# First modulation by chunks of channels, with the first weight slots worked between them

## The reference

```python
silu_c, silu_cc = silu(c), silu(c_ctx)
mod   = silu_c  @ ada_w[0] + ada_b[0]        # for the 256 tokens of x
mod_c = silu_cc @ ada_w[0] + ada_b[0]        # for the 256 tokens of ctx
sh_m, sc_m, g_m, sh_f, sc_f, g_f = split(mod, 6)
h  = rmsnorm(x,   norm_mix_w[0]) * (1 + sc_m)  + sh_m
hc = rmsnorm(ctx, norm_mix_w[0]) * (1 + scc_m) + shc_m
p, pc = h @ ab_w_in, hc @ ab_w_in            # 1024 -> 2560: u, v, q, k, v of the attention
...
k_mem, v_mem = mem @ xa_w_k[0], mem @ xa_w_v[0]    # used by a later layer
```

## Time and profile before

| | us |
|---|---|
| median of three runs | 2557.49 |
| the profiled execution's own time | 2559.29 |
| its span in the trace | 2557.3 |
| TensorE busy | 2496.8 |
| VectorE busy | 1989.3 |
| ScalarE busy | 1175.6 |

### The profile page before, as it was taken

How to read it: one execution, slowest core, us unless ns; L and a number is a source line. 1 busy time by engine, 2 the same in 40 slices (tenths; PEclk the granted TensorE clock), 3 DMA queues, 4 the chain that set the end, 5 groups by cost and what they waited for, 6 DMA issues and landing times.

```text
span 2557.3 us, 41955 instructions
## 1 busy us (share of the span) xinstructions
PE 2496.8 (98%) x16459; PEld 2145.1 (84%) x16459; DVE 1989.3 (78%) x2455; ACT 1175.6 (46%) x1498; POOL 89.2 (3%) x116
## 2 busy tenths in 40 slices
PE   7999999999999999999999899999999999999998
PEld 5877788888889998889999688888888888888886
DVE  2886877777767886757887748888888888988887
ACT  3435200001421005531014736777777777777776
POOL 0100100000000001000002000000000000000000
PEclk8999999999999999999999999999999999999999
DMA  8843444453335553334554035999899989999996
GB/s 333 313 168 126 167 172 167 167 172 116 116 108 218 181 180 141 108 108 160 185 181 185 16 115 194 374 363 374 334 375 366 366 340 373 366 351 357 364 373 252
DMA packets 91397, 602.74 MB, mean 236 GB/s; under 512 B 9840, under 2 KB 12912, under 8 KB 24688
## 3 DMA queue, kind: packets, MB, share of 16 engines
q1 hardware_dynamic: 76848, 540.05, 55.9%
q0 software_dynamic: 14400, 60.56, 6.7%
HBM read 598.47 MB, written 2.10 MB: 235 GB/s over the span
## 4 chain that ended last, share of the span: by engine, by line
PE 92%; DVE 4%; ACT 2%; issue 1%; DMA 1%; SPq 0%; DVEq 0%; ACTq 0%
PE bank L1188 12%; PE bank L1191 12%; PE bank L1192 12%; PE bank L2492 8%; PE bank L2496 8%; PE bank L2495 8%; PE bank L2527 4%; PE bank L2523 4%; PE bank L2526 4%; PE bank L535 2%; PE bank L1425 1%; PE bank L1446 1%; ACT arena L1470 1%; PE bank L2505 1%; PE bank L1176 1%; PE bank L1238 1%
## 5 line engine op out<-in xcount | busy, mean ns | idle before, releaser
L984 DVE TENSOR_TENSOR ring_part<-ring,arena_part 128x2048 fp32r<-128x2048 f32 x481 | 1079.9, 2274 | 29.7 <-ACT arena_part L1003 13.5
L2848 ACT ACTIVATE arena_part<-ring 128x2048 fp32r<-128x2048 f32 x339 | 647.0, 1920 | 192.7 <-DMA ring<-in_stream 192.4
L1188 PE MATMUL bank<-arena_part 128*128 128x256 f32 (+1 forms) x2040 | 652.2, 320 | 7.6 <-DVE ring_part L984 7.6
L1192 PE MATMUL bank<-arena_part,ring_part 128*128 128x256 f32 (+1 forms) x2040 | 648.6, 318 | 0.0
L1191 PE MATMUL bank<-h_part,arena_part 128*128 128x256 f32 (+1 forms) x1496 | 474.9, 317 | 0.0
L1188 PEld LDWEIGHTS bank<-arena_part 128*128 128x128 f32 x2040 | 390.7, 192 | 38.0 <-issue 11.3
L1192 PEld LDWEIGHTS bank<-arena_part,ring_part 128*128 128x128 f32 x2040 | 390.6, 191 | 25.8
L2492 PE MATMUL bank<-arena_part,h_part 128*128 128x512 f32 x896 | 354.2, 395 | 0.0
L2496 PE MATMUL bank<-arena_part,h_part 128*128 128x512 f32 x896 | 349.6, 390 | 0.0
L2495 PE MATMUL bank<-ring_part,h_part 128*128 128x512 f32 x896 | 348.9, 389 | 0.0
L1292 ACT ACTIVATE arena<-bank 128x256 f32<-128x256 f32 (+1 forms) x66 | 30.1, 456 | 636.6 <-PE bank L1192 635.6
(11 more groups left out here) (376 smaller groups left out, 3071.2 us busy)
## 6 DMA issues: line engine op xcount, KB each, us to landing
ring<-in_stream SPq DMA_DIRECT2D x511, 1024.0 KB, 4.9
arena<-in_ada_stream POOLq DMA_DIRECT2D x80, 512.0 KB, 4.4
consts<-in_mem_w POOLq DMA_DIRECT2D x8, 512.0 KB, 4.1
consts<-in_small POOLq DMA_DIRECT2D x1, 2800.0 KB, 11.7
arena<-in_c_rows POOLq DMA_DIRECT2D x2, 1024.0 KB, 6.9
arena<-in_ab_bias POOLq DMA_DIRECT2D x1, 2048.0 KB, 8.5
arena<-in_t_bias POOLq DMA_DIRECT2D x1, 2048.0 KB, 7.9
arena<-in_mem_t SPq DMA_DIRECT2D x1, 1024.0 KB, 4.9
```

Source lines behind the costliest of these rows:

```text
L984: return nc.vector.tensor_tensor(low, value, high.bitcast(F32), ALU.subtract)
L1188: m = nc.tensor.matmul(out_ap, w_high, high, start=start, stop=False)
L1192: return nc.tensor.matmul(out_ap, w_low, high, start=False, stop=stop)
L2848: nc.scalar.activation(high, ring[:, where], ACT.Copy).then_inc(sem("moe_high"), 1)
```

## The change

- `START` has only K0a, K0b, V0a, V0b. The 8 MB of shift and scale weights are laid out anew, `ada_mix`: one MB for each 128 *output* channels of shift and of scale together, with all 1024 input channels. SP loads them into ring rooms 0 to 3 behind AB0 and AB1, each behind a wait of its own.
- `ada_products(c)` makes shift and scale of one chunk of channels: eight matmuls of 256 columns with 32 stationary columns (two used, the rest zero). ScalarE copies the bank out (`copy_rows`), `fold_rows(c)` adds the four groups and turns them in two small matmuls with the constant `fold`, and VectorE's `first_scale(c)` adds the bias and makes the scale.
- `first_products(k)` does the 96 matmuls of AB0 and AB1 with the four output tiles side by side, twelve matmuls for each chunk, between `ada_products(c + 3)` and `fold_rows(c + 2)` of later chunks.
- Rounding and splitting of AB0 and AB1 comes before the modulation, that of AB2 and AB3 stands amid the eight chunks. The 24 later chunks are spread over AB4 to AB9. The memory values use banks 4 and 5 and are copied out earlier.

The pieces of the diff stand in the order TensorE, ScalarE, VectorE, SP.

```diff
-START = ["K0a", "A0", "A1", "K0b", "A2", "A3", "V0a", "A4", "A5", "V0b", "A6", "A7"]
+START = ["K0a", "K0b", "V0a", "V0b"]
...
+            mem_value_products()
...
+            for c in range(DC):
+                pe.wait_ge(sem("squared"), bk.up("squared"))
+                m = group_sums(sums, sqv[:, c, :], TT, c == 0, c == DC - 1)
+            m.then_inc(full(sums), 1)
+            ada_products(0)
+            ada_products(1)
             mem_value_products()
+            fold_rows(0)
             rstd_pe(bk, TT)
+            fold_rows(1)
+            ada_products(2)
...
+            for c in range(DC):
+                if c + 3 < DC:
+                    ada_products(c + 3)
+                if c + 2 < DC:
+                    fold_rows(c + 2)
+                first_products(c)
...
+            for c in range(DC):
+                if c + 3 < DC:
+                    copy_rows(c + 3)
+                for s in range(2):
+                    t = slice(SEQ * s, SEQ * (s + 1))
+                    scaled_act(bk, c == DC - 1 and s == 1, spread_last)
+                    nc.scalar.activation(ab_high[:, c, t], hv[:, c, t], ACT.Identity, bias=shift(0, 0, c, s))\
+                        .then_inc(sem("in_high"), 1)
+                if c in (3, 5):
+                    slot_high_act(bk, AB_AT + 2 + (c == 5), ab_slot_high, fresh=True)
...
+                if c in (4, 6):
+                    slot_low_dve(bk, AB_AT + 2 + (c == 6), ab_slot_high)
...
-            for n in range(2, 7):
-                first_chunks(3 * n - 6, 3 * n - 3)
+            for n, chunks in ((4, (0, 5)), (5, (5, 9)), (6, (9, 12))):
+                first_chunks(*chunks)
                 slot_low_dve(bk, AB_AT + n, ab_slot_high)
...
+            for n in range(2, RING):
+                load(n)
+            for j in range(DC):
+                if j >= ADA_ROOMS:
+                    sp.wait_ge(*marks["ada_made"][j - ADA_ROOMS])
+                elif j == ADA_ROOMS - 1:
+                    for made in marks["values_full"]:
+                        sp.wait_ge(*made)
+                else:
+                    sp.wait_ge(sem("slots_used"), j + 2)
```

More of the change, by code:

```diff
@@ L1919, in _, with ada_products, fold_rows @@
             pe.wait_ge(sem("silu_c_ready"), 1)
[L1921 to L1935, removed]
             pe.wait_ge(sem("mem_split"), DC)
             mem_key_products(range(2, 4))
-            ada_products(2)
+            mem_value_products()
+            rows_copied, ada_made = [], []
+            marks["ada_made"] = ada_made
+            def ada_products(c):
+                b = bk.fill(ADA_BANKS[c % 2])
+                rows_copied.append(bk.freed(bk.turn - 1))
+                pe.wait_ge(free(b), bk.emptied())
+                pe.wait_ge(sem(f"ada_landed{c % ADA_ROOMS}"), 16 * (c // ADA_ROOMS + 1))
+                room = ring[:, c % ADA_ROOMS * SLOT:(c % ADA_ROOMS + 1) * SLOT]
+                for late in range(2):
+                    for g in range(4):
+                        k = 4 * late + g
+                        m = nc.tensor.matmul(PS[b][32 * g:32 * g + 32, X2], silu_c[:, k, :],
+                                             room[:, k * SEQ:(k + 1) * SEQ], start=not late, stop=bool(late))
+                m.then_inc(full(b), 1)
+                ada_made.append((full(b), bk.filled()))
+            def fold_rows(c):
+                pe.wait_ge(*rows_copied[c])
+                b = bk.fill(FOLD_BANK)
+                pe.wait_ge(free(b), bk.emptied())
+                for n in range(2):
+                    m = nc.tensor.matmul(PS[b][:, 4 * c + 2 * n:4 * c + 2 * n + 2], ada_rows[c % 4][:, n * P:(n + 1) * P],
+                                         small_at("fold")[:, 0:2], start=True, stop=True)
+                m.then_inc(full(b), 1)
+            sums = bk.next_bank()
             for c in range(DC):
@@ L1942, in _ @@
             m.then_inc(full(sums), 1)
-            ada_products(3)
+            ada_products(0)
+            ada_products(1)
             mem_value_products()
+            marks["values_full"] = [(full(b), bk.filled_in[b]) for b in MEM_BANKS]
+            fold_rows(0)
             rstd_pe(bk, TT)
[L1946 to L1962, removed]
@@ L2618, in _, with copy_rows @@
             root_act(bk, TT, 0)
[L2619 to L2627, removed]
+            for n in range(2):
+                slot_high_act(bk, AB_AT + n, ab_slot_high, fresh=True)
+            def copy_rows(c):
+                b = bk.fill(ADA_BANKS[c % 2])
+                act.wait_ge(full(b), bk.filled())
+                nc.scalar.activation(ada_rows[c % 4], PS[b][:, X2], ACT.Copy).then_inc(free(b), 1)
+            copy_rows(0)
+            copy_rows(1)
             for n in range(4):
                 bk.fill(MEM_BANKS[n % 2])
+            b = bk.fill(MEM_BANKS[0])
+            act.wait_ge(full(b), bk.filled())
+            nc.scalar.activation(mem_made_values(0), PS[b][:, :], ACT.Copy).then_inc(free(b), 1)
+            bk.fill(MEM_BANKS[1])
+            bk.turn += 1
+            spread_last = bk.freed(bk.turn - 1)
+            copy_rows(2)
+            for c in range(DC):
[8 more added lines that the diff above has]
+                    slot_high_act(bk, AB_AT + 2 + (c == 5), ab_slot_high, fresh=True)
+            for _ in range(DC):
+                bk.fill(FOLD_BANK)
             def silu_rows(rows, times):
@@ L2645, in _ @@
                 to(uT[:, g, :], ACT.Gelu_apprx_tanh)
[L2646 to L2649, removed]
+            for n in range(4, 6):
+                slot_high_act(bk, AB_AT + n, ab_slot_high, used=AB_AT + 3)
             for t in range(4):
```

156 lines of the change are left out of this document (101 added, 55 removed).

## The result

The changed kernel takes 2567.39 us (median), the kernel before 2557.55 beside it on the same chip: the ratio is 1.0036, with a 95% interval from 1.0027 to 1.0046. That is 9.8 us slower. The profiled execution took 2569.23 us, 9.9 more than that of before.

What follows compares the result with a forecast made beforehand. TensorE was taken to bound the kernel, with VectorE's chain 1.4 us behind at the gate. Gate 2.5 us later plus 2.4 of cold clock gave +4.9: 2562.4 us against the median of 2557.5, range 2554 to 2569.

Steps and rivals of the forecast that it cites:

- the sum: Whole kernel: gate begins 2.5 us later, cold clock behind it costs 2.4, everything after as before; +4.9 us.
- rival D: Loop: POOL's 3.5 MB of loads collide with modulation chunks 5 to 7; +8.4 us, 2565.9; chance 0.08.
- rival A: Whole kernel: the sum holds, with or without either cold stretch; -3 to +8 us around +4.9; chance 0.75.
- two cold stretches: Half clock at the loop's first chunk (0 to 3.4 us, 1.7 taken) and behind the gate's wait (1.7 to 3.4, 2.4 taken).
- B: TensorE's head start reaches the end, with VectorE's chain ending 7 us sooner; -6 us, 2551.4; chance 0.10.
- C: TensorE's clock is at half through the loop, pitch 8.7 us; +15 us, 2577; chance 0.07.
- without the gap of 2.91 us it keeps the full clock: Start, K0b's products: TensorE goes on at once from K0a, so 48 matmuls at full clock end at 22.7.
- The one half-speed stretch that I did allow for: Loop's first chunk, after TensorE's idling from 41.7 to 46.5: a loss between 0 and 3.4 us, 1.7 taken.
- VectorE's chain after it: 78.4: VectorE's 24 later chunks, first to last: 78.4 us against 80.6 before, with about 5 us of waiting for a chunk.
- The steps of the pitch: Each loop turn: modulation products, copy, two roundings and handoffs take 2.5 us, twelve matmuls 2.73; pitch 5.3 us.
- by it the loop would be at half speed throughout: Loop: the prediction's reading of the skill page on throttling in waiting loops, against which it set the attention's full clock.
- Costed at nothing: Third and fourth SP waits, splits from AB4 on (AB8's tightest), and moved value copies (0.6 us each): no cost.

Runs made afterwards that it cites:

- e1: Changed kernel with the gate's weights in a room of their own, loaded amid the 24 chunks, not after the last: 2559.30 us, ratio 1.0008.
- e8: Changed kernel with 18 small matmuls on constants ahead of the loop, where TensorE waits for the fourth modulation chunk: 2564.45 us, ratio 1.0030.
- e12: Changed kernel with only the portions of the 24 later chunks between VectorE's slots changed, to 4, 3, 3, 3, 4, 4, 3: 2569.48 us, ratio 1.0046.
- e5_three: Changed kernel with gate's weights loaded early, ScalarE's copy behind the rounding, and `silu_rows` moved behind the fifth chunk's rounding: 2554.92 us, ratio 0.9986.
- e10_two: Changed kernel with the gate's weights loaded early and ScalarE's copy behind the rounding: 2553.04 us, ratio 0.9982.
- e2: Changed kernel with ScalarE's `copy_rows(c + 3)` behind the two roundings of chunk c, not ahead of them: 2563.92 us, ratio 1.0022.
- e11: e10_two with the 24 later chunks in portions 4, 3, 3, 3, 4, 4, 3 between VectorE's slots: 2556.21 us, ratio 0.9992.
- e3: Changed kernel with `silu_rows` moved from behind the last rounding to behind the fifth chunk's, so VectorE starts sooner: 2567.78 us, ratio 1.0043.

## Why the prediction was right, and where it was off

**The mechanism held.** The start of TensorE's stage moved forward, that of VectorE's back, and the gate's weights, loaded behind VectorE's last chunk, became the wait. e1 shows it: with the weights early and nothing else changed, 7.6 us come back. The size did not hold: the sum said +4.9, and it was +9.4, nearly twice as much. That the time lies in the range (to 2569) is partly luck, since the range was widened for rival D, which did not occur; rival A, the sum, was given 2556 to 2567 and in other places at most +8 or +8.5, and its own two cold stretches at their longest add only 2.7 to the 4.9. One sign failed as well: the gate's matmuls were to begin between 163 and 168 and began at 172.58. Another held barely, the 85.8 us from VectorE's first chunk to the landed weights, where 80 to 86 were given. Rivals B, C and D did not occur as told: TensorE's head start did not reach the end (B), the loop did not run at half speed (C), and no turn behind the first waited for a modulation chunk (D). (B's price does not follow from its condition: at a pitch of 4 us the prediction's own steps put AB2 near 76 to 78, not at 81.5.)

**The sizes, in the order of the sum.**

| step | predicted | measured |
|---|---|---|
| fourth modulation chunk landed | 44.0 | 46.6 |
| first products | 46.5 | 49.90 |
| pitch of the loop | 5.3 | 5.3 (first turn 6.8) |
| AB2 begun | 83.0 | 86.35 |
| VectorE's first chunk | 83.4 | 86.70 |
| from there to the end of the last chunk | 78.4 | 81.3 |
| from there to the weights landed | 4.5 | 4.5 |
| TensorE's wait at the gate | 7 | 8.1 |
| gate's products begin | 166.3 (+2.5) | 172.58 (+8.8) |
| cold clock behind it | 2.4 | 1.7 |

Two terms were mis-sized. They add up: the start of VectorE's chain 3.3 later, the chain 2.9 longer, the cold clock 0.7 less, so 4.9 + 3.3 + 2.9 - 0.7 = 10.4, and the traces have 10.5. The first step is "without the gap of 2.91 us it keeps the full clock": that gap closed, but TensorE waited 2.10 us at V0a, and behind it the clock was 0.50 for 3.4 us. The prediction's own times hold this wait (K0b's products end at 22.7, V0a is split at 24.4), but it charges nothing for the clock behind it. This cost 1.7; together with V0a's start at 24.96 instead of 24.4 (VectorE copies a memory key out in between, L3063 at 24.44) it moved the sums and V0b, behind which SP may issue the fourth modulation chunk, and with that the whole loop. The one half-speed stretch that I did allow for came as well (1.93 for 1.07, 6.76 for 5.31: 2.3 us, where 1.7 was taken; e8's median fell by 2.5, with its share of chance). In all 3.4 us, and since VectorE's chain hangs on the loop's end they arrive at the gate in full.

The second is "VectorE's chain after it: 78.4", where the wait for chunks was put at 5 us. It was 8.4, in five places; the rest of the chain was 0.5 shorter than summed. The even portions (e12) took the waits for chunks away and the chain was no shorter, since ScalarE's rounding of AB6, which TensorE's progress sets, took their place. So the term was mis-sized because I added up VectorE's own work and one known wait. It left out the four further waits for chunks (4.5 us), and also that a slot in mid-chain has a time before which it cannot be split: in the changed kernel that rounding ended at 121.6 and VectorE came to AB6 at 122.18, so without the 3.3 us of waits for chunks ahead of it VectorE would have stood there for 2.7 of them. Behind that point the one long wait, for a chunk behind the load of constants, is 3.92 in the changed kernel and 4.8 and 5.1 in e5_three and e10_two. In e12_even that chunk was issued 12 us behind the constants (128.69, not 3 us as in the changed kernel) and VectorE did not wait for it.

**The loop.** The steps of the pitch (copy 0.46 ahead of two roundings, 1.2 us of waiting less what the fold fills) were right: 0.76 of waiting by the trace, and with the copy behind the rounding the pitch fell by 0.9. Weighed against it was the page TensorE: Matmul & The Clock Gate of the Trainium skill, section "HAM oscillation — how this bites in real kernels", whose case is a loop that waits in each turn for longer than it works and starts each turn cold. The waits here are much shorter than the work, so "by it the loop would be at half speed throughout" asked more of that page than it says. The trace of the changed kernel shows full speed (1.00 from 53 to 60) with waits of 0.76 in 5.3 us; single waits of about 2 us had a cold stretch behind them at 25 and 46.

**Costed at nothing.** SP's waits and the value copies cost nothing that shows. AB8's split was late by 1.5 and took that from the wait at the gate, as the prediction said it would; in e10_two, where that wait is gone, it is 1.9 us on the path.

**Where the head start of 13 us went.** By AB2 1.3 us were left: AB0 and AB1 with the modulation between them last 36.5 us (49.90 to 86.35), before 24.6. The groups by line (count, busy us, mean ns, idle before) for that stretch of the changed kernel:

```profile
L1981 PE MATMUL bank<-arena_part 128*128 128x512 f32 x32 | 14.2, 445 | 4.3 <-ACT arena_part L2681 4.3
...
L1937 PE MATMUL bank<-ring,rstd 128*32 128x256 f32 x64 | 4.3, 385 | 0.0
L1947 PE MATMUL bank<-consts,arena 128*128 128x2 f32 x20 | 3.0, 255 | 0.7 <-DVE mod L3091 0.7
```

The 96 matmuls at 0.23 are 21.8, the waits 4.3 and 0.7, the chunk matmuls 4.3, the folds 3.0, the cold first turn 1.5: 35.6, which leaves 0.9 of 36.5 without an account. The order alone gives back 0.9 us in each of four turns, 3.6 us, by the pitch of e2; its median fell by 3.0.

## What to carry over

When work is brought forward on one engine, follow the resource that the next meeting point waits for back to *its* engine, and see whether that engine's start moved too; here it moved the other way, and the smallest repair was to free the load from that chain (7.6 us for a few lines). A chain of one engine that takes things from others is not the sum of its own work: look for the pieces in it that something else sets, because time gained ahead of them is lost there. In e11 and e12 that was a slot's rounding (5.9 and 6.3 us of waiting), in e3 a chunk's landing (4.55 us). And in a loop that hands over each turn, what is for a later turn belongs behind what the other engine waits for now.

## What was not expected of the hardware

- The same wait had a stretch at 0.50 behind it in some traces and none in others. TensorE waited 2.0 to 2.1 us near 25 in all eleven traces of the changed kernel and its versions: eight have the stretch, e5_three, e8_filler_start and e10_two have none. Near 46 the wait was 2.0 to 2.2 us. The five traces with the copy ahead of the rounding and no filler have a stretch at 0.50 there, in two of them only from about 49 on; the four with the copy behind it and no filler have none. A loop idle 0.76 of each 5.3 us ran at 1.00. What decides is open.
- The 512 KB of the gate's weights took 4.2 us to land, with DMA idle before it and 2 MB issued 0.5 us behind it. Of the 512 KB chunk loads some took 5.3 to 7.7 us beside others, and one that was issued 3 us behind the load of constants 12.2 us.
- Kernels with nearly the same work differ in the spread of their executions: 3.4 us for the kernel before (21 executions), 7.2 for e5_three and 8.6 for e11_two_even (11 each). Stretches of half clock near 25 and near 1400 differ between their traces; whether they are all of it is open.
